# Seven products on token halves for half of a's rows, with weight sums by accumulating DMAs

## The chip, the core and the metric

The kernel runs on one core of one Trainium2 chip. The metric is the device time of one execution in microseconds; the median of 3 runs before the change is 2513.88 us.

## What is computed

Two layers of a model run one after the other on 512 tokens of 2048 channels, all in float32. Only the first part of the first layer matters here:

```python
h = rmsnorm(x, norm_g)
proj = jnp.einsum('bld,dn->bln', h, w_in)
v, bg, cg, za, u, zb, ga, gb = jnp.split(proj, SPLITS, axis=-1)
ya = bg * causal_depthwise_conv(cg * v, conv_w)
ya = jnp.einsum('blc,cd->bld', ya * jax.nn.silu(za), w_out_a)
yb = jax.nn.gelu(s5_scan(u, a_re, a_im, log_dt, b_re, b_im, c_re, c_im, d_skip))
```

The four parts v, cg, bg and za have 2048 channels each, and together they are "a". After them come the gate of the scan's output, the output projections, and the whole second layer; the change leaves those as they are but for their first loads and waits.

## The kernel before

Activations lie channel by token: a tile has 128 channels on the partitions and 512 tokens. Every matmul operand is split into a high part (rounded to the format TensorE takes, `hH`, `WH`) and a low part (the rest, `hL`, `WL`), and each product is three matmuls (`triple`, L560): high by high, high by low, low by high, added in PSUM.

The work is cut into **units**. A unit is one weight chunk of 128 x 1024 (512 KB): eight blocks of 128 x 128 for one output tile and half of the 2048 input channels, so 8 x 3 = 24 matmuls of 512 columns. An output tile (a projection) takes two units, kc 0 and 1. `Plan` (L69) writes the list of all units: u (8 tiles), zb (8), the gates ga and gb (32), then a in 16 blocks c of four tiles, then the rest. The first two u tiles are interleaved (kc 0 of both, then kc 1 of both); all others are in sequence.

Five queues go through the same list of units, each with a function `unit()`: SyncE loads the raw chunk into a ring of three slots `W` (`fetch`, L365), as soon as VectorE is done with the slot; ScalarE writes `WH` two units ahead (`hi`, L930, L936), when TensorE has left the buffer; VectorE writes `WL` (`lo`, L1304, L1307); TensorE waits for it (L557) and multiplies. Three buffers of `WH` and `WL` exist. Within a queue the order is the order in the program, so whatever stands between two calls of `unit()` delays the next split.

Around the change:

- At the start h is first computed without the token's factor (L998, L1602). VectorE and TensorE form the factor `RSA` meanwhile. POOL then scales x by it (L2181 to L2184), ScalarE writes the high parts again (`normed`, L1016, L1019) when the last u tile has read the old ones, and VectorE the low parts (L1634, L1636). The first zb tile waits for them, k by k (`n_ready`, L684).
- Beside the units runs the scan of u. `ssm_phases(n)` (L348) says how many of its phases each queue has done by unit n: one parameter piece per unit for units 4 to 24 (VectorE, `ssm_params`, L1413), then 130 phases up to the end of a's block `SSM_C` = 12 (units 28 to 199). In them POOL makes tables (L2138 to L2141), VectorE forms and scans (L1549 to L1578), TensorE drives and reads out (L603, L615).
- For each block c of a, the four tiles come as v, cg, bg and za; ScalarE copies the first out of PSUM (L1056), VectorE multiplies, convolves with three taps and multiplies (L1672 to L1691), ScalarE applies silu (L1061), and SyncE stores the product in DRAM (L454).

## Time and profile before

| | |
|---|---|
| median of 3 runs | 2513.88 us (2513.25 to 2514.46) |
| the profiled execution | 2516.84 us |
| its span | 2515.6 us |
| mean granted clock of TensorE | 0.998 |
| busy: TensorE, VectorE, ScalarE, POOL | 2496.6, 1592.1, 857.1, 369.9 us |
| bytes moved | 353.08 MB, mean 140 GB/s |

The durations of matmuls in the profile overlap, since the next one starts before the last has left the array; the distance between starts is what a matmul costs. The profile has one execution, 3 us above the median.

### The profile page before, as it was taken

To read this page: it belongs to the slowest core of one execution; us is meant where nothing else is said; L and a number is where in the kernel's file an instruction comes from. 1 tells how busy PE (TensorE), PEld (TensorE's weight loads), DVE (VectorE), ACT (ScalarE), POOL (GpSimd) and SP (SyncE) were. 2 spreads that over 40 slices of the span, in tenths; PEclk is the share of its full clock that TensorE was granted. 3 is DMA by queue.
4 is the path that set the end of the run, shared out by engine and by line. 5 is a ranking of instruction groups with operands and counts; after the bars stand their busy time and mean duration, and the time that the engine had idled before them with its cause. 6 is when DMAs were issued, how large, how long until landed. Compare 5 with 4: busy or idle time off the path is not lost.

```text
span 2515.6 us, 30050 instructions
## 1 busy us (share of the span) xinstructions
PE 2496.6 (99%) x11932; PEld 2158.8 (86%) x11932; DVE 1592.1 (63%) x2161; ACT 857.1 (34%) x1171; POOL 369.9 (15%) x286
## 2 busy tenths in 40 slices
PE   9899999999999999999999999999999999999998
PEld 8788888888888888888888888878888888888888
DVE  7976666668777777743756666557566564467534
ACT  5322222222222222223432223333465664324432
POOL 2133343334333343100000000000000000000001
PEclk9999999999999999999999999999999999999999
DMA  5243433333333333333576667524322222556333
GB/s 195 90 147 132 138 136 129 135 121 124 98 126 115 114 116 110 108 105 109 188 253 228 226 233 235 184 90 154 106 84 84 85 77 91 190 169 209 126 126 126
DMA packets 117964, 353.08 MB, mean 140 GB/s; under 512 B 15424, under 2 KB 18752, under 8 KB 117824
## 3 DMA queue, kind: packets, MB, share of 16 engines
q1 hardware_dynamic: 117824, 351.16, 41.5%
q8 instruction: 94, 1.54, 0.2%
q14 instruction: 46, 0.38, 0.0%
HBM read 321.68 MB, written 23.07 MB: 137 GB/s over the span
## 4 chain that ended last, share of the span: by engine, by line
PE 96%; DVE 2%; DMA 1%; ACT 0%; SPq 0%; issue 0%; DVEq 0%; ACTq 0%
PE bank L561 28%; PE bank L563 28%; PE bank L562 28%; PE bank L764 2%; PE bank L765 2%; PE bank L763 2%; PE bank L817 1%; PE bank L807 1%; PE bank L624 1%; PE bank L727 1%; PE bank L612 1%; DMA W<-in_w 1%; DVE WL L1307 0%; DVE SM L1394 0%; PE bank L800 0%; PE bank L798 0%
## 5 line engine op out<-in xcount | busy, mean ns | idle before, releaser
L1307 DVE TENSOR_TENSOR WL<-W,WH 128x1024 fp32r<-128x1024 f32 (+1 forms) x452 | 585.9, 1298 | 563.4 <-ACT WH L936 561.8
L936 ACT ACTIVATE WH<-W 128x1024 fp32r<-128x1024 f32 (+1 forms) x452 | 473.8, 1050 | 953.6 <-PE bank L563 671.7
L561 PE MATMUL bank<-hH,WH 128*128 128x512 f32 x1792 | 682.6, 381 | 8.6 <-DVE hL L1636 5.7
L563 PE MATMUL bank<-hH,WL 128*128 128x512 f32 x1792 | 680.5, 380 | 0.0
L562 PE MATMUL bank<-hL,WH 128*128 128x512 f32 x1792 | 680.4, 380 | 0.0
L561 PEld LDWEIGHTS bank<-hH,WH 128*128 128x128 f32 x1792 | 339.5, 189 | 67.8 <-issue 13.1
L563 PEld LDWEIGHTS bank<-hH,WL 128*128 128x128 f32 x1792 | 339.4, 189 | 48.4
L562 PEld LDWEIGHTS bank<-hL,WH 128*128 128x128 f32 x1792 | 339.6, 190 | 47.5
L561 PE MATMUL bank<-h2H,WH 128*128 128x512 f32 x624 | 239.6, 384 | 0.1
L562 PE MATMUL bank<-h2L,WH 128*128 128x512 f32 x624 | 236.5, 379 | 0.0
L563 PE MATMUL bank<-h2H,WL 128*128 128x512 f32 x624 | 236.5, 379 | 0.0
L2138 POOL TENSOR_TENSOR TAB<-E,W 128x512 f32<-128x512 f32 x64 | 84.0, 1313 | 537.9 <-DVE V L1576 519.4
L561 PEld LDWEIGHTS bank<-h2H,WH 128*128 128x128 f32 x624 | 117.9, 189 | 18.2 <-issue 1.4
L563 PEld LDWEIGHTS bank<-h2H,WL 128*128 128x128 f32 x624 | 117.9, 189 | 16.7
L562 PEld LDWEIGHTS bank<-h2L,WH 128*128 128x128 f32 x624 | 118.0, 189 | 15.8
L2141 POOL TENSOR_TENSOR TAB<-TAB,T 128x512 f32<-128x512 f32 x64 | 123.6, 1931 | 5.0
L1323 DVE SCALAR_TENSOR_TENSOR ACC<-W,SC,ACC 128x1024 f32<-128x1024 f32 x90 | 115.1, 1279 | 1.0 <-DMA W<-in_ada 0.6
L2192 POOL TENSOR_SCALAR YK<-X,PC,ST 128x512 f32<-128x512 f32 x16 | 12.8, 802 | 632.8 <-DVE X L1769 632.8
L763 PE MATMUL bank<-WH,h2H 128*128 128x512 f32 x256 | 97.6, 381 | 0.0
L561 PE MATMUL bank<-AH,WH 128*128 128x512 f32 x256 | 97.2, 380 | 0.0
L561 PE MATMUL bank<-mH,WH 128*128 128x512 f32 x256 | 97.2, 380 | 0.0
L562 PE MATMUL bank<-AL,WH 128*128 128x512 f32 x256 | 97.0, 379 | 0.0
(306 smaller groups left out, 3534.2 us busy)
## 6 DMA issues: line engine op xcount, KB each, us to landing
W<-in_w SPq DMA_DIRECT2D x332, 512.0 KB, 3.6
W<-in_ada SPq DMA_DIRECT2D x96, 512.0 KB, 4.1
W<-in_wa SPq DMA_DIRECT2D x32, 512.0 KB, 4.2
W<-in_wo SPq DMA_DIRECT2D x32, 512.0 KB, 3.7
W<-in_wvv SPq DMA_DIRECT2D x32, 512.0 KB, 4.1
W<-in_wb SPq DMA_DIRECT2D x16, 512.0 KB, 4.5
URAW<-U SPq DMA_DIRECT2D x96, 64.0 KB, 3.1
scr_ga<-SO SPq DMA_DIRECT2D x16, 256.0 KB, 2.0
```

The lines of the kernel that those rows point to most:

```text
L561: e.matmul(o, wh, xh, start=first, stop=False)
L562: e.matmul(o, wh, xl, start=False, stop=False)
L563: return e.matmul(o, wl, xh, start=False, stop=last)
L612: mm = e.matmul(bank[b + z][:, :], BSTK[:, s, z, :], pairs(USTK[:, s, :]), start=True, stop=True)
L763: e.matmul(o, h2H[:, k, q4[q]], wh, start=k == 0, stop=False)
L764: e.matmul(o, h2H[:, k, q4[q]], wl, start=False, stop=False)
L765: mm = e.matmul(o, h2L[:, k, q4[q]], wh, start=False, stop=k == 15)
L936: e.activation(chunk_parts(n)[0][:, c], W[:, i % NW, c], ACT.Copy).then_inc(sem["hi"], 1)
L1307: e.tensor_tensor(wl[:, c], W[:, plan.item_of[n] % NW, c], wh[:, c].bitcast(F32), ALU.subtract).then_inc(sem["lo_v"], 1)
L1323: e.scalar_tensor_tensor(out=acc[:, :], in0=w, scalar=c, in1=acc[:, :], op0=ALU.mult, op1=ALU.add).then_inc(sem["ada_v"], 1)
L2138: e.tensor_tensor(o, er_, wi if part else wr, ALU.mult).then_inc(sem["ssm_p"], 1)
L2141: e.tensor_tensor(o, o, y, ALU.add if part else ALU.subtract).then_inc(sem["ssm_p"], 1)
```

## The change

Three parts.

**The products.** For the blocks c = 8 to 15 of a, the 512 tokens and the 2048 input channels are each taken as two halves, and the four tiles as two pairs j, (cg, v) and (bg, za), by `ST_PARTS`. Each pair by both halves of channels is a 2 x 2 grid of weight chunks b11, b12, b21, b22, and each pair's result on both token halves is formed from seven products in place of eight. A unit i of a block is one product of 24 matmuls with 256 columns, for pair j = i % 2, so a block has 14 units in place of 8. The sums of the weights are not computed by an engine: for units 0 to 3 and 6 and 7 SyncE loads a plain chunk (`base`), and for units 4, 5 and 8 to 13 POOL issues a DMA with `accum_op=ALU.add`, which adds another chunk to what the slot holds, when VectorE has split the chunk before. Six raw slots are used, three of them new (`WX`). The sums of the tokens are formed once, in block c = 7, by VectorE and ScalarE (`factor_sums`), and the fourth goes in the place of the second token half of `hH` and `hL` for channels 0 to 1023. The partial results lie in three PSUM banks per pair, are copied out in the middle of the accumulation by ScalarE, and added by VectorE in `corner_11`, `corner_12` and `corner_22`.

**The scan** has to be finished before block 8: `SSM_C` is 6 in place of 12, so the same 130 phases go into units 28 to 151.

**The head.** The last two u tiles and the first two zb tiles are interleaved like the first two u tiles (`two_rows`, `project_two`). POOL's 16 scalings of x are VectorE's (`scaled_rows`), and the high and low parts are written in four groups of four with a `unit()` between.

The diff, cut to its core:

```diff
-SSM_C = 12
+SSM_C = 6
+ST_C = 8
+ST_PARTS = ((2, 0), (1, 3))
+ST_SLOTS = (0, 0, 1, 1, 0, 0, 2, 2, 0, 0, 2, 2, 0, 0)
...
+        self.two_rows("u", [[w1[64 + m, c] for c in range(2)] for m in range(2)])
+        for m in range(2, 6):
+            self.proj("u", [w1[64 + m, c] for c in range(2)])
+        self.two_rows("u", [[w1[64 + m, c] for c in range(2)] for m in (6, 7)])
+        self.two_rows("zb", [[w1[72 + m, c] for c in range(2)] for m in range(2)])
         for m in range(2, 8):
-            self.proj("u", [w1[64 + m, c] for c in range(2)])
-        for m in range(8):
             self.proj("zb", [w1[72 + m, c] for c in range(2)])
         for m in range(32):
             self.proj("gate", [w1[80 + m, c] for c in range(2)])
-        for c in range(16):
+        for c in range(ST_C):
             for part in (0, 2, 1, 3):
                 self.proj("a", [w1[16 * part + c, kc] for kc in range(2)])
+        self.strassen_units(w1)
...
+    def strassen_units(self, w1):
+        self.first_after = i0 = len(self.items)
+        slots = [[i0 % NW, (i0 + 1) % NW], [(i0 + 2) % NW, 3], [4, 5]]
+        user = dict(self.ring_user)
+        base, sums = [0] * 6, [0] * 6
+        for c in range(ST_C, 16):
+            n0 = len(self.item_of)
+            self.strassen[c] = n0
+            b = [[[w1[16 * part + c, kc] for part in ST_PARTS[j]] for kc in range(2)] for j in range(2)]
+            for i in range(14):
+                n, j = n0 + i, i % 2
+                s = slots[ST_SLOTS[i]][j]
+                self.item_of.append(None)
+                self.slot_of[n] = s
+                (b11, b12), (b21, b22) = b[j]
+                raw, added = ((b11, None), (b21, None), (None, b12), (b22, None), (None, b22), (None, b12),
+                              (None, b21))[i // 2]
+                if raw is not None:
+                    base[s] += 16
+                    self.base[c, i] = (s, raw, user.get(s))
+                    self.arrives[n] = ("base", s, base[s])
+                else:
+                    sums[s] += 16
+                    self.sums[c, i] = (s, added, user[s])
+                    self.arrives[n] = ("sum", s, sums[s])
+                user[s] = ("unit", n)
+            slots = slots[1:] + slots[:1]
...
+    def two_rows(self, stage, srcs):
+        n = [self.chunk(srcs[m][c]) for c in range(2) for m in range(2)]
...
+    def slot_free(user):
+        kind, i = user
+        return lo_done[i] if kind == "unit" else (sem["ada_v"], i + 1)
...
+    def r_bank(c, r, j):
+        return bank[(0, 1, 2, 4, 5, 6)[r + 3 * j] if r or c % 2 == ST_C % 2 else (3, 7)[j]]
+    MC = [SI[:, i // 2, half[i % 2]] for i in range(4)]
...
+        def base(c, i):
+            s, src, user = plan.base[c, i]
+            if user is not None:
+                e.wait_ge(*slot_free(user))
+            elif s > NW:
+                e.wait_ge(*nth("st_l", 0))
+            e.dma_start(raw_chunk(plan.strassen[c] + i), src).then_inc(w_base[s], 16)
+        def store_product(c):
+            e.wait_ge(*product_done[c])
+            e.dma_start(scratch["am"][c], SO[:, c % 2, :]).then_inc(spilled[c % 2], 16)
...
+        for c in range(ST_C):
             for _ in range(8):
                 ssm_until(unit())
-            e.wait_ge(*nth("a_v", c))
-            e.dma_start(scratch["am"][c], SO[:, c % 2, :]).then_inc(spilled[c % 2], 16)
+            if c < ST_C - 1:
+                store_product(c)
+        for i in (0, 1, 2, 3, 6, 7):
+            base(ST_C, i)
+        store_product(ST_C - 1)
+        for c in range(ST_C, 16):
+            if c < 15:
+                base(c + 1, 0)
+                base(c + 1, 1)
+            if c > ST_C:
+                store_product(c - 1)
+            if c < 15:
+                for i in (2, 3, 6, 7):
+                    base(c + 1, i)
+            for _ in range(14):
+                unit()
+        store_product(15)
...
+        def project_two(ps, XH, XL, ready=None, beside=None):
+            for kc in range(2):
+                for p in ps:
+                    n = unit()
+                    if beside is not None:
+                        beside(n)
+                    products(n, p, kc, 0, 15, XH, XL, ready if p == ps[0] else None)
...
-        for p in u_p[2:]:
+        for p in u_p[2:6]:
             project(p, xh, xl, beside=norm)
+        project_two(u_p[6:], xh, xl, beside=ssm_until)
         def n_ready(k):
             e.wait_ge(*nth("xl", 16 + k))
 
-        for i, p in enumerate(spill_p + a_p):
-            project(p, xh, xl, n_ready if i == 0 else None, beside=ssm_until)
+        project_two(spill_p[:2], xh, xl, n_ready, beside=ssm_until)
+        for p in spill_p[2:] + a_p:
+            project(p, xh, xl, beside=ssm_until)
+        first_half = lambda x, k0: (lambda k: x[:, k0 + k, half[0]])
+        second_half = lambda x, k0: (lambda k: x[:, k0 + k, half[1]])
+        whole = lambda x: (lambda k: x[:, k, :])
+        factors = [(first_half(hH, 0), first_half(hL, 0)), (first_half(hH, 8), first_half(hL, 8)),
+                   (whole(S1H), whole(S1L)), (second_half(hH, 0), second_half(hL, 0)),
+                   (whole(S2H), whole(S2L)), (whole(S3H), whole(S3L)), (second_half(hH, 8), second_half(hL, 8))]
+        def strassen_product(c, i):
+            f, j, g = i // 2, i % 2, c - ST_C
+            n = unit()
+            r = (0, 1, 2, 2, 0, 0, 0)[f]
+            if f == 0:
+                if c == ST_C:
+                    for w in conv_read[0] if j == 0 else [nth("skip", 7)]:
+                        e.wait_ge(*w)
+                elif c == ST_C + 1:
+                    e.wait_ge(*nth("skip", 7))
+                else:
+                    e.wait_ge(*nth("st_v", g - 2, (8, 13)[j]))
+            elif f == 1:
+                for w in [nth("st_v", g - 1, (1, 2)[j])] if g else conv_read[1] if j == 0 else []:
+                    e.wait_ge(*w)
+            elif f == 2:
+                for w in [nth("st_v", g - 1, (3, 6)[j])] if g else conv_read[2] if j == 0 else []:
+                    e.wait_ge(*w)
+                if g == 0:
+                    e.wait_ge(*nth("st_l", 0))
+            elif f == 3:
+                e.wait_ge(*nth("st_a", g, 3 + j))
+                if g == 0:
+                    e.wait_ge(*nth("s4_l", 0))
+            elif f == 4:
+                e.wait_ge(*nth("st_a", g, 1 + j))
+            elif f == 5:
+                e.wait_ge(*nth("st_a", g, 5 + j))
+            else:
+                e.wait_ge(*nth("st_v", g, (5, 7)[j]))
+            xh_, xl_ = factors[f]
+            o = r_bank(c, r, j)[:, 0:256]
+            for k8 in range(8):
+                w = slice(128 * k8, 128 * k8 + 128)
+                begins = f in (0, 1, 2) and k8 == 0
+                ends = f in (1, 3, 6) and k8 == 7
+                wh, wl, x_h, x_l = WH[:, n % NB, w], WL[:, n % NB, w], pairs(xh_(k8)), pairs(xl_(k8))
+                e.matmul(o, wh, x_h, start=begins, stop=False, skip_group_check=True)
+                e.matmul(o, wh, x_l, start=False, stop=False, skip_group_check=True)
+                mm = e.matmul(o, wl, x_h, start=False, stop=ends, skip_group_check=True)
+            mm.then_inc(sem["used"], 1)
+        for c in range(ST_C, 16):
+            for i in range(14):
+                strassen_product(c, i)
...
         def normed(k):
-            e.wait_ge(sem["used"], plan.last(u_p[7]) + k // 8)
+            e.wait_ge(sem["used"], plan.units(u_p[7])[k // 8] + 1)
             e.wait_ge(*nth("xn", k))
...
+        for i in range(4):
+            for k in range(4 * i, 4 * i + 4):
+                normed(k)
+            ssm_until(unit())
+        spill(0)
+        spill(1)
+        for s in range(2, len(spill_p)):
+            ssm_until(unit())
+            ssm_until(unit())
+            spill(s)
...
+        for c in range(ST_C, 16):
+            g = c - ST_C
+            for i in range(14):
+                if i in (1, 2, 5, 6, 9, 10):
+                    j = (i - 1) % 2
+                    m = j + 2 * (4 < i < 8)
+                    unit_done(c, i - 1)
+                    if i == 1 and g == 0:
+                        e.wait_ge(*nth("s4_l", 0))
+                    if g > 0 and i < 8:
+                        e.wait_ge(*nth("st_v", g - 1, (3, 6, 5, 7)[m]))
+                    if i > 8:
+                        e.wait_ge(*nth("st_v", g, 1 + j))
+                    e.activation(MC[m], r_bank(c, 2 if 4 < i < 8 else 0, j)[:, 0:256],
+                                 ACT.Copy).then_inc(sem["st_a"], 1)
+                unit()
...
+        def scaled_rows(ks):
+            for k in ks:
+                e.wait_ge(*nth("xsq", k))
+                e.wait_ge(*nth("xl", k))
+                e.tensor_tensor(XS[:, k, :], XS[:, k, :], RSA[:, :], ALU.mult).then_inc(sem["xn"], 1)
+        for m in range(3, 6):
             ssm_until(unit())
             if m == 4:
                 e.wait_ge(*nth("rsa", 0))
-                for i in range(4):
+                for i in range(2):
                     keep_u(i)
+            if m == 5:
+                keep_u(4)
+                scaled_rows(range(4))
             ssm_until(unit())
             if m == 3:
                 inv_rms(0, 3, 0, 0)
-            else:
-                keep_u(m)
+            if m == 4:
+                keep_u(2)
+                keep_u(3)
+            if m == 5:
+                scaled_rows(range(4, 8))
+        for i in range(4):
+            ssm_until(unit())
+            if i == 0:
+                keep_u(5)
+            scaled_rows(range(8 + 2 * i, 10 + 2 * i))
...
             ssm_until(unit())
-            if s == 0:
-                for k in range(8, 16):
-                    normed(k)
+            if i == 1:
+                keep_u(6)
+                keep_u(7)
...
+        def factor_sums(batch):
+            k, l = slice(4 * batch, 4 * batch + 4), slice(8 + 4 * batch, 12 + 4 * batch)
+            a, b, d, s4 = SX[0][:, :, :], SX[1][:, :, :], SX[2][:, :, :], SX4[batch][:, :, :]
+            if batch:
+                e.wait_ge(*nth("st_l", 0, 3))
+            for x, ks, h in ((a, k, 0), (b, k, 1), (d, l, 1), (s4, l, 0)):
+                e.tensor_tensor(x, f32(hH[:, ks, half[h]]), f32(hL[:, ks, half[h]]),
+                                ALU.add).then_inc(sem["st_x"], 1)
+            yield
+            e.wait_ge(*nth("st_x", 0, 8 * batch + 3))
+            e.tensor_tensor(d, d, b, ALU.subtract).then_inc(sem["st_x"], 1)
+            e.wait_ge(*nth("st_x", 0, 8 * batch + 5))
+            e.tensor_tensor(b, a, b, ALU.subtract).then_inc(sem["st_x"], 1)
+            e.wait_ge(*nth("st_x", 0, 8 * batch + 6))
+            e.scalar_tensor_tensor(out=a, in0=d, scalar=-1.0, in1=a, op0=ALU.mult,
+                                   op1=ALU.subtract).then_inc(sem["st_x"], 1)
+            e.wait_ge(*nth("st_x", 0, 8 * batch + 7))
+            e.scalar_tensor_tensor(out=s4, in0=s4, scalar=-1.0, in1=a, op0=ALU.mult,
+                                   op1=ALU.subtract).then_inc(sem["st_x"], 1)
+            yield
+            for f, (lo_, hi_, x) in enumerate(((S1L, S1H, d), (S3L, S3H, b), (S2L, S2H, a))):
+                e.wait_ge(*nth("st_h", 0, 3 * batch + f + 1))
+                e.tensor_tensor(lo_[:, k, :], x, f32(hi_[:, k, :]), ALU.subtract).then_inc(sem["st_l"], 1)
+            yield
...
+        def corner_22(c, j):
+            g = c - ST_C
+            unit_done(c, 10 + j)
+            e.wait_ge(*nth("st_a", g, 3 + j))
+            if g > 0:
+                e.wait_ge(*nth("st_v", g - 1, (8, 14)[j]))
+            o_ = x22[0] if j == 0 else halves(x22[1])
+            a, b = MC[2 + j], r_bank(c, 0, j)[:, 0:256]
+            e.tensor_tensor(o_, a if j == 0 else tokens(a), b if j == 0 else tokens(b),
+                            ALU.add).then_inc(sem["st_v"], 1)
...
+            if i == 10:
+                corner_12(c, 0)
+                e.wait_ge(*nth("st_v", g, 3))
+                e.wait_ge(*(nth("st_v", g - 1, 11) if g > 0 else nth("a_v", ST_C - 1, 4)))
+                e.tensor_tensor(halves(cv[:, half[0]]), tokens(x11[0]), tokens(x12[0]),
+                                ALU.mult).then_inc(sem["st_v"], 1)
+            if i == 11:
+                corner_22(c, 0)
+                corner_12(c, 1)
+            if i == 12:
+                corner_22(c, 1)
+            if i == 13:
+                unit_done(c, 12)
+                e.wait_ge(*nth("st_v", g, 5))
+                e.tensor_tensor(halves(cv[:, half[1]]), tokens(r_bank(c, 0, 0)[:, 0:256]), tokens(x22[0]),
+                                ALU.mult).then_inc(sem["st_v"], 1)
+                e.wait_ge(*nth("st_v", g, 8))
+                e.wait_ge(*(nth("st_v", g - 1, 14) if g > 0 else nth("a_v", ST_C - 1, 6)))
+                e.tensor_scalar(o, CV[:, 0:512], taps[0], None, ALU.mult).then_inc(sem["st_v"], 1)
+                for x in (1, 2):
+                    e.wait_ge(*nth("st_v", g, 8 + x))
+                    e.scalar_tensor_tensor(out=o, in0=CV[:, x:512 + x], scalar=taps[x], in1=o, op0=ALU.mult,
+                                           op1=ALU.add).then_inc(sem["st_v"], 1)
...
-        e.wait_ge(*nth("rsa", 0))
-        for k in range(16):
-            e.wait_ge(*nth("xsq", k))
-            e.wait_ge(*nth("xl", k))
-            e.tensor_tensor(XS[:, k, :], XS[:, k, :], RSA[:, :], ALU.mult).then_inc(sem["xn"], 1)
-        for n in range(4, plan.units(wg_p[0])[0]):
+        for n in range(4, plan.strassen[ST_C]):
             ssm_until(n)
         for _ in beside:
             pass
+        for c in range(ST_C, 16):
+            for i in (4, 5, 8, 9, 10, 11, 12, 13):
+                s, src, user = plan.sums[c, i]
+                e.wait_ge(*slot_free(user))
+                e.dma_start(raw_chunk(plan.strassen[c] + i), src, accum_op=ALU.add).then_inc(w_sum[s], 16)
```

## Rows read from the trace of the kernel before

**Rows 1.** The page: TensorE's busy time, its clock in 40 slices, the chain

```profile
PE 2496.6 (99%) x11932; PEld 2158.8 (86%) x11932; DVE 1592.1 (63%) x2161; ACT 857.1 (34%) x1171; POOL 369.9 (15%) x286
...
PEclk9999999999999999999999999999999999999999
...
PE 96%; DVE 2%; DMA 1%; ACT 0%; SPq 0%; issue 0%; DVEq 0%; ACTq 0%
```

**Rows 2.** Timeline, TensorE, 512 wide: start, length, engine, line; 73 starts apart

```profile
2459.84 0.38 PE L561 MATMUL bank<-yH,WH 128*128 128x512 f32 x1
...
2475.60 0.38 PE L562 MATMUL bank<-yL,WH 128*128 128x512 f32 x1
```

**Rows 3.** Timeline, TensorE, 256 wide, 48 starts apart

```profile
2485.92 0.28 PE L561 MATMUL bank<-yH,WHX 128*128 128x256 f32 x1
...
2491.28 0.28 PE L561 MATMUL bank<-yH,WH 128*128 128x256 f32 x1
```

**Rows 4.** Windows: length, busy by engine, granted clock, DMA share, GB/s

```profile
400.00:800.00 400.00, 400.00 (x1881) 344.40 (x1880) 290.85 (x330) 103.21 (x129) 143.28 (x100) 1.00 0.36 121
800.00:1000.00 200.00, 200.00 (x941) 172.21 (x940) 153.61 (x175) 50.28 (x61) 72.65 (x52) 1.00 0.34 113
```

**Rows 5.** Groups by form, 560 to 1210 us: busy us, mean ns

```profile
L1307 DVE TENSOR_TENSOR WL<-W,WH 128x1024 fp32r<-128x1024 f32 x122 | 168.6, 1382 | 134.9 <-ACT WH L936 134.3
...
L1557 DVE TENSOR_TENSOR V<-V 128x512 f32<-128x512 f32 x18 | 12.5, 692 | 0.5
...
L936 ACT ACTIVATE WH<-W 128x1024 fp32r<-128x1024 f32 x123 | 129.7, 1055 | 373.6 <-PE bank L563 373.6
```

**Rows 6.** DMA: a window at full load; issues, KB, us to landing

```profile
10.00:12.00 2.00, 2.00 (x11) 1.67 (x11) 1.78 (x3) 1.29 (x3) 0.00 (x0) 1.00 1.06 409
...
W<-in_w SPq DMA_DIRECT2D x332, 512.0 KB, 3.6
...
XS<-in_xT SPq DMA_DIRECT2D x7, 512.0 KB, 8.6
```

**Rows 7.** Chain of waits, 40 to 115 us: start us, length, what

```profile
58.82 1.21 DVE SM L1394
...
95.64 0.61 DVE T L1391
...
99.89 0.69 DVE U L1619
100.59 5.30 DVE hL L1636 x8
105.88 1.14 DVE WL L1307
107.02 0.61 DVE T L1391
...
108.57 0.76 DVE hL L1636
```

**Rows 8.** Waits of TensorE: total us, times, longest

```profile
PE bank L561 <- DVE hL L1636: 5.7, 2, 3.1
```

**Rows 9.** Timeline, TensorE, at 75 us; in brackets its idle time

```profile
75.67 0.48 PE L561 MATMUL bank<-hH,WH 128*128 128x512 f32 x1 [2.63 <-DVE WL L1307]
...
77.88 0.63 PE L561 MATMUL bank<-hH,WH 128*128 128x512 f32 x1
78.31 0.63 PE L562 MATMUL bank<-hL,WH 128*128 128x512 f32 x1
```

**Rows 10.** POOL scaling x, and a small operation of VectorE after it

```profile
L2184 POOL TENSOR_TENSOR XS<-XS,RSA x16: 1267/1276/2265, 53.1 to 73.3; 128x512 f32<-128x512 f32 x16
...
75.95 0.19 DVE L1391 TENSOR_TENSOR SM<-SM,SMI 128x32 f32<-128x32 f32 x1
```

**Rows 11.** Timeline, VectorE: ends of the next parameter piece

```profile
115.01 0.18 DVE L1491 COPY SM<-SM 128x32 f32<-128x32 f32 x1
...
118.22 0.18 DVE L1386 TENSOR_SCALAR SM<-SM 128x32 f32<-128x32 f32 x1
```

More of the change, by code:

```diff
@@ L1663, in dve_program @@
                     ssm_until(unit())
-                if c == 15 and i >= 2:
-                    for k in range(4 * (i - 2), 4 * (i - 2) + 4):
-                        low_y(k)
+                    if c == ST_C - 1:
+                        next(factors, None)
+                if c == ST_C - 1 and i == 3:
+                    last_factor_low(0)
+                    last_factor_low(1)
                 if i == 1:
@@ L1693, in gate_in @@
+        for c in range(ST_C, 16):
+            for i in range(14):
+                unit()
+                if i == 0 and c > ST_C:
+                    gated_conv(c - 1, 14)
+                if i in (3, 4):
+                    corner_11(c, i - 3)
+                if i >= 10:
+                    gated_conv(c, i)
+                if c == 15 and i >= 6:
+                    low_y(i - 6)
+        gated_conv(15, 14)
         def gate_in(i):
```

205 lines of the change are left out of this document (158 added, 47 removed).

## The prediction

> **What bounds the kernel now.** I read the page's busy times first. TensorE is busy for 2496.6 of 2515.6 us, at a granted clock of nine tenths or more in all 40 slices, and the chain that ended last is 96% PE [rows 1]. So the time is the count of matmuls times the interval between their starts, plus the few stalls, and a change pays only if it shortens one of the two.
>
> The interval is in the timeline, not in the durations, which overlap. 512-wide starts lie (2475.60 - 2459.84) / 73 = 0.216 us apart [rows 2]; 256-wide ones, which exist only near the end, (2491.28 - 2485.92) / 48 = 0.1117 us [rows 3]. Half the columns cost a little more than half the time, and the weight load beside each matmul does not show at 256.
>
> The other engines have room, but not everywhere. In the stage of the spilled rows and the first rows of a VectorE is busy 291 of 400 us, later 154 of 200 [rows 4]. Splitting one chunk costs ScalarE 1.06 us and VectorE 1.2 to 1.4 us [rows 5]. In the first 115 us the chain leaves TensorE and runs over VectorE [rows 7]: one stall of 2.63 us at 73 us, and two, 5.7 us in all, before the low parts of the second normalisation [rows 8, 9].
>
> **Part 1, the products: -30.** A unit is 24 matmuls. Before, a channel block c of 8 to 15 is 8 units of 24 x 0.2158 = 5.18 us, 41.4 us. After, 14 units of 24 x 0.1117 = 2.68 us, 37.5 us. Gain 3.9 us, times 8 = 31.3 us.
>
> Work beside it: splits now come every 2.68 us. ScalarE: 14 x 1.06 plus six copies and a gate, some 18 of 37.5 us. VectorE: 14 x 1.2, six corner sums and the convolution, some 24 us (256 wide taken as 0.35 to 0.4, half of the 0.69 of a 512-wide addition [rows 5]). Both fit. Where the two meet: unit 12 of a block overwrites a bank that VectorE must have read, and VectorE queues that read behind the split of unit 13. From the end of unit 10: ScalarE 1.06, VectorE 1.2, sum 0.4 and some 0.1 of signals make 2.8 us, against the 2.68 of unit 11. So 0.13 us of stall per block, 1 us in all. -31.3 + 1 = -30.
>
> **The DMAs** decide whether this holds. Every unit needs 512 KB: 6 plain loads and 8 accumulating ones per block. At full load the engines moved 409 GB/s [rows 6], so 512 KB take 1.28 us. No row shows an accumulating DMA. Lower bound: like a plain one. Upper bound: no row gives one. I take double, 2.56 us, since it reads the weights and the tile. The block then asks for (6 + 16 + 0.5 for the stored product) x 1.28 = 29 of 37.5 us. Latency: a sum starts when the slot's last split is done, 2.4 us into a unit (ScalarE 1.06, VectorE 1.2, signals [rows 5]), and is due four units later, so it may take 4 x 2.68 - 2.4 = 8.3 us. A plain load lands in 3.6 us [rows 6]; plus 1.3 for the second read, plus an estimated 1 on POOL, is 6, and 7.3 when a plain load is between. Cost: 0, covered by these 8.3 us. If the cover is gone, every us later is a us of stall per block, in unit 12 first.
> The Trainium skill, Collectives: The Full Stack, "Why ReduceScatter is half of AllGather", says an add in the DMA path halves the rate because it has two reads; no row here shows it, and it would give the same 2.56 us.
>
> The queues. SP loads units 0 and 1 of the next block first, then waits for the stored product of the block before (about 1 us into the block), and only behind it come units 2, 3, 6 and 7 of the next block, whose slots come free in units 8 to 11; they are due from the next block's start on, 7 us or more later. POOL issues the sums in order of the splits that release them, and behind the scan's tables, which end with c = 6. So neither queue holds a load back: 0.
>
> **Part 2, the head.** POOL loses its 16 scalings of 1.27 us [rows 10]. While they ran, VectorE's 128x32 operations took 1.21 us, else 0.19 [rows 7, 10], and that made the stall at 73 us. It goes: -2.6 us, and the half-speed matmuls behind it too (0.43 us apart [rows 9], some 8 of them, -1.6 us). Sum -4.2.
>
> But VectorE does the scalings itself now, 16 x 0.61 = 10 us (a 512-wide operation [rows 7]), in units 10 to 15, where its parameter pieces, splits and readings of u already fill nearly 24 of 31 us. It comes 1.7 us later to the last piece before unit 16, the one of 4.3 us, and has two scalings behind that. The first low part came 3 us after TensorE wanted it; now 4.3. The pairing doubles the time for each half in principle. But the four groups of low parts are each behind a unit of VectorE's, that is a split and a parameter piece. Group 2: split 1.15, piece 1.55 [rows 7], behind four low parts at 0.67 [rows 7], against half a unit: 2.8 us late. Group 3: a split that waits for the end of unit 16 (2.2 with ScalarE's part), a piece of 3.4 [rows 11], two readings of u, a low part, against 5.2 us of unit 17: 2.5 late. Group 4: four low parts, split, a piece of the same operations (some 2.7, an estimate), a low part, against half a unit: 3.8 late. Stalls: 4.3 + 2.8 + 2.5 + 3.8 = 13.4, less the 5.7 of before: +7.7. One more drop of the clock: +1.6. Between the bounds "both waits hidden" (-5.7) and +12 I take +9.3, as it comes from the same order that gives the old stalls right.
>
> **Part 3, the scan in fewer units.** It must now end with c = 6: 130 phases over 124 units instead of 172. VectorE's busy share less the splits (1.38 of 5.18 us, 0.27) is 0.50 in its later stretch [rows 4, 5], of which the convolution is about 0.1; 0.4 x 172 / 124 = 0.55, so 0.92 in all. It fits, with little left; the last readout lies one unit, not two, behind the phase that it waits for. +2, bounds 0 and +16 (every late readout).
>
> **Part 4, c = 7 and the ends.** The token sums are 22 operations of 1024 elements at 1.15 to 1.2 plus 2 more splits, 28 us beside splits and convolution (14) in 41: a lag of up to 5 us, under the 8 us that a split may come late at 512 width. 0, bound +4. One us for the two ends of the stage.
>
> **Sum:** -30 - 4.2 + 9.3 + 2 + 1 = -22 us. The profiled execution took 2516.84 us (span 2515.6), 3.0 above the median 2513.88; I put the same -22 on the median: 2492 us. Its own range is 2480 to 2505.
>
> **Rivals.**
> **A, sums that land late (slower, 0.27).** Place: the accumulating DMA of unit 13, the last of six in a row, one per 2.68 us. If one costs three plain ones, 3.84 us, the row gains 1.16 us each, and it lands after 6 + 1.3 + 5 x 1.16 = 13 us, plus the next block's loads. Against 8.3 that is 5 to 7 us per block: -30 + 8 x 6 + 8 (parts 2 to 4) = +26, 2540 us. It decides from about 11 us on, where the 30 us less the 8 are used up (3.8 - 1 = 2.8 us per block); then 2514. For it: no row shows such a DMA, and under full load at the start plain loads of 512 KB took 8.6 us to land [rows 6]. Against: a demand of 29 us in 37.5. With the clock falling after each stall, as it did after 2.63 us [rows 9], it could be 2580.
> The same could come from POOL's side: rows 7 and 10 show VectorE and POOL holding each other up, and VectorE is busy two thirds of this stage. One operation of 1.2 us ahead of each issue gives 7.2 to 8.5 us of latency, at most 0.2 us of stall; three give 11. The Trainium skill, SBUF — State Buffer, "SBUF: two separate sides", says that POOL's descriptors wait only for VectorE's two-port operations; the block has one of those, and by that rule nothing is lost.
> **B, VectorE bounds the first 900 us (0.13).** Its slowed operations (a split at 1.38 instead of 1.15 in mean [rows 5]) grow with POOL's share, which rises by 1.39 too. Part 3 at its bound: -22 + 14 + 3 = -5, 2509 us.
> **C, both waits of the head are hidden (0.10).** That is -5.7 - 1.6 instead of +9.3: -38, 2476 us. Against: the order above.
> That the change does not do what it says has no room: 14 products of 256 columns stand in the loop.
>
> **Numbers.** Forecast 0.50. About 0.2% (5 us) is what a measurement tells from none. Faster: 0.48 of the forecast, 0.10 of C, 0.04 of B = 0.62. Same: 0.02 + 0.05 of B + 0.03 of A = 0.10. Slower: 0.04 of B, 0.24 of A = 0.28. The range from 2475 to 2545 leaves out half of A above 2540 and a little of C.
>
> **What would show it.** Right: 256-wide starts 0.112 us apart in the a stage, blocks of about 37.7 us, landing of the accumulating DMAs under 8 us, VectorE's small operations at 0.19 us before 75 us, four stalls before low parts between 98 and 125 us. Wrong: TensorE waiting for splits or corner sums inside the blocks, blocks over 41 us, the chain running over DMA or VectorE in the a stage, no stall at 98 us.

## The result, and the profile after

The changed kernel takes 2498.45 us in the median of four runs (2498.32 to 2498.74); the kernel before, run beside it, takes 2514.17 us. The ratio is 0.9936, interval 0.9919 to 0.9953: 15.7 us or 0.6% faster, where the forecast was 2492 and 22 us. The profiled executions took 2516.84 and 2498.38 us.

The page of the changed kernel: busy times, four lines of the slices, the software DMA queue, the chain by engine.

```profile
span 2497.2 us, 32838 instructions
PE 2469.8 (99%) x13084; PEld 2171.9 (87%) x13084; DVE 1721.4 (69%) x2313; ACT 925.9 (37%) x1267; POOL 410.4 (16%) x334
...
PE   9799999999999999999999999999999999999998
...
DVE  7877889789999875666856666557565554467534
...
PEclk9899999999999999999999999999999999999999
DMA  5244444343333379988676677524222222556333
...
q0 software_dynamic: 9216, 33.56, 7.6%
...
PE 94%; DVE 3%; issue 1%; ACT 1%; DMA 1%; SPq 0%; DVEq 0%; ACTq 0%
```

Against [rows 1] TensorE's busy time fell by 26.8 us and the span by 18.4: more matmul time was saved than reached the end. The second slice shows where the rest went. Its PE digit is 7 and its clock digit 8, and the whole chain has 3% on VectorE, where it had 2% [rows 1]. The slices are 62 us wide, so this is the stretch from 62 to 125 us.

What TensorE waited for in the whole kernel (line, what it waited for, us in total, times, longest):

```profile
PE bank L690 <- DVE hL L1896: 7.7, 2, 4.5
PE bank L690 <- DVE U L1862: 6.6, 1, 6.6
PE bank L794 <- POOL CAU L2577: 2.0, 1, 2.0
PE bank L876 <- DVE T L2035: 1.9, 8, 0.4
```

The two waits for low parts [rows 8] have become 4.5 and 3.2 us, and a new one of 6.6 us stands between them: TensorE waits for VectorE to write U. The stall at 73 us [rows 9] is gone. TensorE's timeline, rows of 512 columns:

```profile
98.16 0.77 PE L690 MATMUL bank<-hH,WH 128*128 128x512 f32 x1 [4.50 <-DVE hL L1896]
98.72 0.63 PE L691 MATMUL bank<-hL,WH 128*128 128x512 f32 x1
99.14 0.63 PE L692 MATMUL bank<-hH,WL 128*128 128x512 f32 x1
...
112.96 0.77 PE L690 MATMUL bank<-hH,WH 128*128 128x512 f32 x1 [6.56 <-DVE U L1862]
...
116.50 0.47 PE L692 MATMUL bank<-hH,WL 128*128 128x512 f32 x1
116.81 0.38 PE L690 MATMUL bank<-hH,WH 128*128 128x512 f32 x1
117.02 0.38 PE L691 MATMUL bank<-hL,WH 128*128 128x512 f32 x1
...
126.03 0.48 PE L690 MATMUL bank<-hH,WH 128*128 128x512 f32 x1 [3.23 <-DVE hL L1896]
```

Behind the first two waits the starts lie 0.43 us apart, half speed, for 13 and 9 matmuls (the first and last of them in part), before they are 0.216 apart again; behind the third, three matmuls run at full speed and then 9 are slow. Against full speed this costs 2.85, 1.9 and 1.7 us, 6.5 us in all. Such a stretch does not follow every wait. In the kernel before, two of three waits had one, of 1.7 us each, and this one had none:

```profile
101.39 0.45 PE L561 MATMUL bank<-hH,WH 128*128 128x512 f32 x1 [3.05 <-DVE hL L1636]
101.68 0.38 PE L562 MATMUL bank<-hL,WH 128*128 128x512 f32 x1
```

VectorE's timeline says why the wait of 6.6 us exists:

```profile
102.69 2.74 DVE L1896 SCALAR_TENSOR_TENSOR hL<-XS,PC,hH 128x512 fp32r<-128x512 f32 x4
107.58 1.23 DVE L1551 TENSOR_TENSOR WL<-W,WH 128x1024 fp32r<-128x1024 f32 x1 [2.15 <-ACT WH L1130]
108.72 0.17 DVE L1734 COPY SM<-SM 128x32 f32<-128x32 f32 x1
...
112.12 1.29 DVE L1862 TENSOR_TENSOR U<-bank,RSA 128x512 f32<-128x512 f32 x2
113.33 2.73 DVE L1896 SCALAR_TENSOR_TENSOR hL<-XS,PC,hH 128x512 fp32r<-128x512 f32 x4
```

Unit 17, the second row of the zb pair, takes the PSUM bank that u row 6 left. VectorE reads that bank (`keep_u(6)`) only after the split of unit 19, which waits for the end of unit 16, and after the parameter piece from 108.7 to 112.1 us. Before, u row 6 was finished one unit earlier (units 12 and 13 instead of 12 and 14) and read at 88.09 us, and its bank was taken one unit later, by unit 18.

In the blocks of seven products the timeline shows 256-wide starts, with one gap per block, before unit 12:

```profile
956.73 0.28 PE L876 MATMUL bank<-S3H,WH 128*128 128x256 f32 x1
...
961.64 0.28 PE L878 MATMUL bank<-S3H,WL 128*128 128x256 f32 x1
962.14 0.35 PE L876 MATMUL bank<-hH,WH 128*128 128x256 f32 x1 [0.22 <-DVE T L2035]
```

Forty-four intervals between the first two rows make 0.1116 us each, as in [rows 3]. The gap from start to start is 0.50 instead of 0.11 us, so it costs 0.39. The gate activation of a block comes every 38.00 us (1002.73, 1040.73, 1078.73 us), against 41.43 us per block before (192 starts; the gate activations behind the scan, at 1131.21 and 1172.65 us, lie 41.44 apart): 8 x 3.43 = 27.4 us.

The accumulating DMAs, by their line (durations on POOL in ns, then landing):

```profile
L2588 POOL DMA_DIRECT2D W<-in_w x35: 858/865/1028, 889.3 to 1176.8; - x35
...
DMA to landing us min/median/max: 5.3/6.0/8.0
```

The landing times are of all 64 sums, in `W` and `WX`. The one that can delay unit 12 is the sum of unit 13, the last of six. It landed in 6.0 to 7.5 us; the 8.0 was a sum of unit 5. How long it may take is in the timelines: its issue, and the split that uses it, which starts when TensorE has freed the buffer.

```profile
951.23 0.86 POOL L2588 DMA_DIRECT2D WX<-in_w  x1 [1.13 <-DVE WL L1551]
...
959.33 1.07 ACT L1130 ACTIVATE WH<-WX 128x1024 fp32r<-128x1024 f32 x1 [0.89 <-PE bank L878]
```

That is 8.1 us, in the last block too (1179.23 to 1187.33), where the sum landed after 7.5.

The stretch from 900 to 1180 us of the kernel before (busy time of PE, PEld, DVE, ACT, POOL, then clock, DMA share, GB/s):

```profile
900.00:1180.00 280.00, 280.00 (x1311) 242.24 (x1311) 166.77 (x189) 66.66 (x75) 49.07 (x34) 1.00 0.33 110
```

and the same stretch of the changed kernel:

```profile
900.00:1180.00 280.00, 278.44 (x2480) 277.31 (x2479) 170.54 (x205) 133.28 (x167) 53.54 (x62) 1.00 0.90 196
```

The DMA engines are busy 90% of this stage, nearly full, and yet TensorE loses 1.6 us of 280.

### The profile page after: what moved, and what is told of

The parts are those of the page before. It is cut to its first block, busy times and chain, and to the rows that moved or that the text cites. A ratio compares the mean times of both kernels' runs of the same rounds, so it can differ in the third digit from the quotient of the medians.

```text
span 2497.2 us, 32838 instructions
## 1 busy us (share of the span) xinstructions
PE 2469.8 (99%) x13084; PEld 2171.9 (87%) x13084; DVE 1721.4 (69%) x2313; ACT 925.9 (37%) x1267; POOL 410.4 (16%) x334
## 4 chain that ended last, share of the span: by engine, by line
PE 94%; DVE 3%; issue 1%; ACT 1%; DMA 1%; SPq 0%; DVEq 0%; ACTq 0%
PE bank L690 24%; PE bank L691 24%; PE bank L692 24%; PE bank L876 4%; PE bank L878 4%; PE bank L877 4%; PE bank L958 2%; PE bank L959 2%; PE bank L960 2%; PE bank L1012 1%; PE bank L1002 1%; DVE WL L1551 1%; DMA W<-in_w 1%; PE bank L762 1%; ACT WH L1130 1%
## 5 line engine op out<-in xcount | busy, mean ns | idle before, releaser
L690 PE MATMUL bank<-hH,WH 128*128 128x512 f32 x1280 | 489.7, 383 | 15.1 <-DVE hL L1896 7.7
L691 PE MATMUL bank<-hL,WH 128*128 128x512 f32 x1280 | 487.6, 381 | 0.0
L692 PE MATMUL bank<-hH,WL 128*128 128x512 f32 x1280 | 487.1, 381 | 0.0
L692 PEld LDWEIGHTS bank<-hH,WL 128*128 128x128 f32 x1280 | 243.3, 190 | 35.0
L691 PEld LDWEIGHTS bank<-hL,WH 128*128 128x128 f32 x1280 | 243.5, 190 | 34.2
L876 PE MATMUL bank<-hH,WH 128*128 128x256 f32 x512 | 141.5, 276 | 1.9 <-DVE T L2035 1.9
L877 PE MATMUL bank<-hL,WH 128*128 128x256 f32 x512 | 140.8, 275 | 0.0
L878 PE MATMUL bank<-hH,WL 128*128 128x256 f32 x512 | 140.8, 275 | 0.0
L2541 POOL TENSOR_TENSOR TAB<-TAB,T 128x512 f32<-128x512 f32 x64 | 113.5, 1773 | 5.0
L1551 DVE TENSOR_TENSOR WL<-WX,WH 128x1024 fp32r<-128x1024 f32 x53 | 65.0, 1226 | 54.0 <-ACT WH L1130 54.0
```

The costliest lines, as they stand in the source:

```text
L690: e.matmul(o, wh, xh, start=first, stop=False)
L691: e.matmul(o, wh, xl, start=False, stop=False)
L692: return e.matmul(o, wl, xh, start=False, stop=last)
L876: e.matmul(o, wh, x_h, start=begins, stop=False, skip_group_check=True)
L877: e.matmul(o, wh, x_l, start=False, stop=False, skip_group_check=True)
L878: mm = e.matmul(o, wl, x_h, start=False, stop=ends, skip_group_check=True)
```

## The experiments

Two theories stood after this reading: that the products bring 27 us and the head takes 9 to 10 back, and that the loss is elsewhere (denser scan, accumulating DMAs, ends of the stage). Ratios are to the kernel before, run in the same rounds (its medians there: 2515.4 to 2516.6 us). Differences to the changed kernel are between medians of different rounds, where the kernel before took 2514.17 us, so they can be off by 1 to 2.5 us.

**The head of before, with the products.** Edit: plan, TensorE, ScalarE and VectorE loops of the head and POOL's scalings as in the kernel before; the rest as changed.

```diff
-        for m in range(2, 6):
+        for m in range(2, 8):
             self.proj("u", [w1[64 + m, c] for c in range(2)])
-        self.two_rows("u", [[w1[64 + m, c] for c in range(2)] for m in (6, 7)])
-        self.two_rows("zb", [[w1[72 + m, c] for c in range(2)] for m in range(2)])
-        for m in range(2, 8):
+        for m in range(8):
             self.proj("zb", [w1[72 + m, c] for c in range(2)])
...
```

> The changed kernel with the head of before: u and zb one row after the other, the scalings on POOL, the readings of u where they were. Theory (products -27.4, head +9): the two parts add up, so this is the changed kernel less 9 us, 2489.5, ratio to before 0.9902; stalls of 2.6 us at 73 us and 5.7 us before low parts as in before, no wait of 6.6 us for a bank, blocks c = 8 to 15 still 38.0 us. By the sum of the prediction (head +5.1) it would be 2493. Rival (the head is harmless, the missing microseconds are lost elsewhere, for instance where the scan has fewer units): the same time as the changed kernel, 2498.

2487.91 us, ratio 0.989 [0.9877, 0.9904]: 27.7 us less than before and 10.5 less than the changed kernel. The waits are those of before (low parts 5.7 us in 2; a split 2.6), and blocks last 38.0 us. The products alone bring the 27.4 us that their blocks show; within the interval nothing is lost at the ends of the stage.

**The new head alone,** on the kernel before.

> The kernel before with the head of the change alone (rows 6 and 7 of u and 0 and 1 of zb in pairs, the scalings on VectorE, the readings of u in their new places); no Strassen, the scan in as many units as before. Theory (the head costs 9 us by itself): 9 us slower than before, ratio 1.0036, with the waits 4.5, 6.6 and 3.2 us near 98, 113 and 126 us. Rival (the head costs only beside the denser scan or the other loads of the changed kernel): no change, ratio 1.000.

2525.40 us, ratio 1.0036 [1.0023, 1.0048], 9.65 us slower than before. Its waits:

```profile
PE bank L567 <- DVE hL L1676: 8.6, 3, 4.5
PE bank L567 <- DVE U L1642: 6.6, 1, 6.6
```

The waits of 4.5, 6.6 and 3.2 us are there without any product or denser scan, and one of 0.93 us more, before low parts at 103.31 us: here the half-speed stretch behind the first wait has 8 slow starts and not 13, and TensorE comes early enough to wait again. Behind the 3.2 us there is no slow stretch. The head costs this by itself, and -27.7 + 9.65 = -18.0 agrees with the -15.7 measured, given intervals of 3 to 4 us either way. It is one bundle: no run has the pairing without the scalings on VectorE.

**Reading u rows 6 and 7 earlier.**

```diff
+            if i == 1:
+                keep_u(6)
+                keep_u(7)
             ssm_until(unit())
-            if i == 1:
-                keep_u(6)
-                keep_u(7)
```

> The changed kernel with the readings of u rows 6 and 7 (keep_u) before the split and the parameter piece of their unit instead of behind them. Theory (unit 17 waits 6.6 us for the bank of u row 6 alone): that wait goes; low parts 8 to 11 come 1.3 us earlier and then stall unit 18 by 1.2 us, low parts 12 to 15 stall by 4.1 instead of 3.2 us; with a little of the clock back, 4.5 to 6 us less than the changed kernel, 2493. Rival (unit 17 is also held by its split or by other low parts, the bank is only the last in name): under 1 us less.

2492.61 us, ratio 0.9908 [0.9894, 0.9921], 5.8 us less than the changed kernel. The wait for U is gone, and those for low parts are now 10.4 us in 4 instead of 7.7 in 2. It was the bank that held unit 17; part of the time went to the next low parts (1.5 us more at 113 us, 3.6 at 120 us), as worked out.

**Plain DMAs in place of accumulating ones.**

```diff
-                e.dma_start(raw_chunk(plan.strassen[c] + i), src, accum_op=ALU.add).then_inc(w_sum[s], 16)
+                e.dma_start(raw_chunk(plan.strassen[c] + i), src).then_inc(w_sum[s], 16)
```

> The changed kernel with the 64 accumulating DMAs turned into plain ones on the same queue, at the same places and with the same waits; it leaves out the second summand of the seven weight sums, so rows c = 8 to 15 of a are not the reference's. Theory (the DMAs are covered): no change of time, within 1 us of the changed kernel; landing falls from 6.0 us to about 4.5, the queue's share of the engines to about half. Rival (the accumulation in SBUF slows splits or matmul operands in the blocks, 38.0 instead of 37.7 us each): 2 to 3 us less.

2498.73 us, no change. The line that issues the DMAs, as above:

```profile
L2588 POOL DMA_DIRECT2D W<-in_w x35: 527/527/751, 888.6 to 1176.1; - x35
...
DMA to landing us min/median/max: 3.6/4.4/5.3
```

the queue, on its page:

```profile
q0 software_dynamic: 9216, 33.56, 4.2%
```

and the stretch from 900 to 1180 us:

```profile
900.00:1180.00 280.00, 278.40 (x2479) 277.27 (x2479) 170.82 (x206) 133.29 (x168) 33.35 (x61) 1.00 0.61 197
```

The queue's share of 16 engines falls from 7.6 to 4.2% of the span: 2.97 us of all engines for one accumulating DMA of 512 KB, 1.64 for a plain one. The blocks stay at 38.0 us, so a DMA share of 0.90 or 0.61 makes no difference to TensorE here, where nothing lands late.

**The corner sum ahead of the split.**

```diff
+                if i == 11:
+                    corner_22(c, 0)
                 unit()
...
-                corner_22(c, 0)
                 corner_12(c, 1)
```

> The changed kernel with the corner sum that frees the bank of unit 12 put before VectorE's split of unit 13 instead of behind it. Theory (unit 12 waits 0.22 us per block for that sum, because the sum queues behind a split that itself waits for the end of unit 10): the eight waits go, 1.8 us less, 2496.7; blocks 37.8 us. Rival (unit 12 or 13 then waits for its split instead, as the sum now delays it): no change.

2498.72 us, no change: the rival. Unit 12 no longer waits, but unit 13 does:

```profile
965.12 0.35 PE L876 MATMUL bank<-hH,WH 128*128 128x256 f32 x1 [0.22 <-DVE T L2035]
```

Its bank is freed by the sister sum, which queues behind the split of unit 14 in the same way. The 0.39 us in front of unit 12 had hidden that; it now stands in front of unit 13, and the blocks last 37.97 us. With both sums moved (below) the blocks take 37.52 us.

**The scan in fewer units, alone,** in the kernel before (`SSM_C = 12` becomes 6).

> The kernel before with the scan to be done with channel block 6 instead of 12 (130 phases over 124 units instead of 172), nothing else. Theory (VectorE has room, no wait of TensorE seen between 140 and 892 us in the changed kernel): 0, within 1 us of before. By the sum of the prediction +2, at its bound +16, 2530.

2515.97 us, ratio 1.000 [0.9991, 1.0009]. VectorE's share rises to what it is in the changed kernel (371 of 400 us busy between 400 and 800, [rows 4] had 291), and TensorE waits for nothing there.

**Sums that are released later.** Three runs, one, two or three units later:

```diff
-                e.wait_ge(*slot_free(user))
+                e.wait_ge(*slot_free((user[0], user[1] + 1)))
```

> The changed kernel with each of the 64 accumulating DMAs issued two units (5.4 us) later: POOL waits for the split of the unit two behind the one that frees the slot. Theory (a late sum holds the splits, and these have two more units less their own 2.3 us before TensorE needs them, so the cover is 8.3 + 3.1 = 11.4 us and not the 8.3 of the prediction): a landing of 6.0 us still fits in the 6.0 us that are left, so 0 to 8 us more than the changed kernel, under 2507. Rival (the prediction's cover of 8.3 us): 2.9 us are left, 3.1 us are lost at least three times per block, 74 us more, 2573.

> The same, three units (8.0 us) later. Theory (cover 11.4 us): 3.4 us are left for a landing of 6.0, so 2.6 us are lost in each of the three steps from sum to sum of a block, units 4, 8 and 12: some 8 us per block, 64 us in all, 2562, more where the clock falls behind the stalls. Rival (cover 8.3 us): 5.7 us at each step, 17 per block, 2635.

2658.32 us (ratio 1.0567) and 2922.23 us (1.1614), 20 and 53 us more per block. Both theories fell: a cover of 11.4 us gave at most 2507 and 2562, one of 8.3 us gave 2573 and 2635. Both had added up single steps, though a sum released two units late waits for the split of a unit that itself waits for a sum (the sum of unit 10 for the split of unit 8, that of 12 for 10). And 65 us of the first run's waits were `T`, the corner sum behind the split of unit 13, the place the prediction had named (51 us more were splits). These two runs show the place; the size of the cover, 8.1 us, is from the trace of the changed kernel above.

> The changed kernel with each accumulating DMA issued one unit (2.7 us) later. After the runs with two and three units: theory now (the sum of unit 13 has a cover of 8.3 us, because its split stands ahead of the corner sum that unit 12 waits for; the other seven have 11.4): unit 13 has 5.6 us left for a landing of 6.0 to 6.8 us, a queue model of the block with these gives 0.9 to 2.5 us per block, 7 to 20 us in all, 2505 to 2519. Rival (all eight have 11.4 us, the losses of the two runs come only from sums that wait for one another): nothing lost, 2499. Other rival (all eight have 8.3 us): 0.4 to 1.2 us in each of three steps, but TensorE waits before units 4, 8 and 12 alike.

2570.68 us, ratio 1.0222 [1.0206, 1.0237]: 9.0 us per block, over 3 times the upper end of the model. TensorE's waits in it:

```profile
PE bank L876 <- DVE T L2035: 41.6, 8, 6.2
PE bank L876 <- DVE WL L1551: 8.0, 12, 1.6
```

POOL's timeline in one block:

```profile
952.50 0.86 POOL L2588 DMA_DIRECT2D W<-in_w  x1 [8.82 <-DVE WL L1551]
953.96 0.86 POOL L2588 DMA_DIRECT2D WX<-in_w  x1 [0.60 <-DVE WL L1551]
955.52 0.86 POOL L2588 DMA_DIRECT2D W<-in_w  x1 [0.69 <-DVE WL L1551]
...
965.89 0.86 POOL L2588 DMA_DIRECT2D WX<-in_w  x1 [1.73 <-DVE WL L1551]
```

and the split of unit 13 in ScalarE's timeline, 7.8 us behind its issue:

```profile
973.70 1.06 ACT L1130 ACTIVATE WH<-WX 128x1024 fp32r<-128x1024 f32 x1 [2.68 <-DMA WX<-in_w]
```

Three releases come in a bunch, behind a split of unit 5 that waited for its own sum. The first of the three, issued at 952.50, landed after 5.6 us, the third (unit 10's, 955.52) after 7.7. Unit 10's split had to wait for it:

```profile
963.28 1.06 ACT L1130 ACTIVATE WH<-W 128x1024 fp32r<-128x1024 f32 x1 [1.02 <-DMA W<-in_w]
```

That split releases unit 13's sum, so this one was issued late too, and landed 7.8 us after its issue at 965.89. Over the eight blocks unit 13's sums took 7.8 to 9.5 us, where the changed kernel has 6.0 to 7.5. Waits for `T` and splits are 49.6 us, 47.7 more than the 1.9 of the changed kernel; 21 of the other 24 us are 198 starts of matmuls that lie up to twice as far apart (granted clock 0.94 between 890 and 1260 us). What kind of queueing lengthens the landing was not separated.

**Products for four blocks only** (`ST_C = 8` becomes 12).

> The changed kernel with the products for channel blocks 12 to 15 only (ST_C = 12), blocks 8 to 11 with 512 columns again. Theory (the gain is 3.4 us per block and linear in the blocks): four blocks fewer give back 13.7 us, 2512 us; the four that are left last 38.0 us each. Rival (part of the gain or loss sits at the ends of the stage or in the room that the freed DMA time gives): more than 3 us off that.

2512.49 us, ratio 0.9984 [0.9975, 0.9993]: 14.0 us more than the changed kernel by the medians, 12.1 by the ratios, so 3.0 to 3.5 per block. Within what rounds differ by, the gain is linear in the blocks.

**A version with the head put right.**

```diff
+PARAM_LATE = {14: 1, 15: 2, 16: 3, 17: 4, 18: 4, 19: 4, 20: 3, 21: 3, 22: 2, 23: 2, 24: 1}
...
-        for i in range(4):
-            for k in range(4 * i, 4 * i + 4):
+        for ks in ((4, 8), (8, 16), (), ()):
+            for k in range(*ks) if ks else ():
                 normed(k)
...
-            while done[0] < ssm_phases(n):
+            while done[0] < ssm_phases(n) - PARAM_LATE.get(n, 0):
...
+            if i == 3:
+                keep_u(6)
+            if i >= 2:
+                for k in range(4 * (i - 2), 4 * (i - 2) + 4):
+                    normed(k)
...
+                if i in (11, 12):
+                    corner_22(c, i - 11)
                 unit()
```

> The changed kernel with three things moved: low parts ahead of the parameter pieces of units 14 to 17 on VectorE, these pieces being made up for by unit 25; the high parts for the second normalisation 4, 4 and 8 in a row on ScalarE, ahead of the splits that wait for TensorE; the readings of u rows 6 and 7 ahead of unit 17 and behind the low parts; both corner sums that free a bank ahead of the split. Theory (each wait of the head is VectorE's order, not its load): the waits near 98, 113 and 126 us and the half-speed matmuls behind them go, 14.3 us of waits and 2 to 4 us of clock, and 2 us in the blocks: 2479 to 2482. Rival (VectorE has no room for the deferred pieces before the scan begins): the waits come back between 120 and 170 us, 2488 or more.

2479.34 us, ratio 0.9852 [0.9839, 0.9865]: 19.1 us less than the changed kernel by the medians (21 by the ratios) and 37 less than before. Its waits:

```profile
PE bank L751 <- DVE BSTK L1769: 3.5, 1, 3.5
PE bank L795 <- POOL CAU L2586: 2.0, 1, 2.0
```

The stretch of the head in it (columns as above):

```profile
95.00:105.00 10.00, 10.00 (x48) 8.77 (x47) 8.44 (x12) 6.55 (x10) 0.00 (x0) 1.00 0.33 107
105.00:115.00 10.00, 10.00 (x49) 8.74 (x47) 8.74 (x23) 2.30 (x5) 0.00 (x0) 1.00 0.33 103
```

Against the same stretches of the changed kernel:

```profile
95.00:105.00 10.00, 6.74 (x19) 5.02 (x20) 9.83 (x16) 2.26 (x4) 0.00 (x0) 0.66 0.14 52
105.00:115.00 10.00, 3.44 (x12) 2.50 (x12) 7.21 (x22) 3.51 (x5) 0.00 (x0) 0.74 0.16 52
```

TensorE runs through at full clock. The waits were in VectorE's order and not in its load, but one of 3.5 us has appeared at 144 us, before the scan's first drive. The moves were made together; apart from the reading of u, above, what each brings was not measured.

> The version with the three things moved (x9_best), and in addition the low parts of the first two B stacks two parameter pieces earlier on VectorE. Theory (its one wait of 3.5 us, before the first drive of the scan at 144 us, is for those stacks, which queue behind the pieces that are made up for): the wait goes with the clock behind it, 4 to 5 us less, 2474 to 2476. Rival (VectorE itself is late at that place, by its load): the wait moves to the first readings of the scan or to the splits near 160 us, 1 us less at most.

Edit: `stack_low(0)` and `stack_low(1)` at parameter piece 15 instead of 17. 2478.76 us, ratio 0.9857 [0.984, 0.9873], the same within the interval. The wait moved, as the rival had it:

```profile
PE bank L691 <- DVE WL L1556: 3.6, 2, 2.6
```

The stack was only the last in a queue. VectorE is busy 53.2 of the 60 us from 140 on, so there its load is probably the bound; no run takes work away from it there.

## Why the prediction was right and where it was off

- **Products, -30: measured -27.4 to -27.7.** Interval, unit and count were right. The term that was mis-sized is the stall before unit 12: 0.13 us forecast, 0.39 measured from start to start (2.1 us over eight blocks); some 0.1 us per block more lies right behind it, at the first matmuls of units 12 and 13. Its mechanism, the corner read queued behind the split of unit 13, was right; that unit 13 has the same wait right behind it was not seen.
- **DMAs at nothing: right.** Landing 6.0 us in the median where 6 to 7.3 was forecast. Unit 13's sums took up to 7.5 us, and the forecast 8.3 that they may take is 8.1 in the trace: it held by 0.6 us, a margin that the cost of 0 does not show. An accumulating DMA takes 1.81 times the engine time of a plain one beside it (2.97 to 1.64 us). The forecast had 2.56 to 1.28, so the factor of two held and both prices were too low: the stage asks for 90% of the DMA engines, not the forecast 29 of 37.5 us, 77%. The Trainium skill, Collectives: The Full Stack, "Why ReduceScatter is half of AllGather", says of that collective that its add halves the rate by needing two reads; 1.81 agrees with that roughly. POOL's issues took 0.86 us with a largest of 1.03, beside a VectorE busy 61% of the time, so none was held up by an operation of 1.2 us. The Trainium skill, SBUF — State Buffer, "SBUF: two separate sides", has POOL's descriptors wait only for VectorE's two-port operations; these issues do not contradict it, and no run puts it to the test.
- **Head, stall at 73 us gone: right** (-2.6, and VectorE's small operations at 0.17 to 0.19 us once POOL does no scalings).
- **Head, four stalls of 4.3, 2.8, 2.5 and 3.8: two came in place and size** (4.50 and 3.23), both with some luck. The 4.3 does not follow from the terms beside it: 3.05 of before, 1.7 later, two scalings 1.2, less a reading of u 0.6, make 5.3. In the traces VectorE begins the last piece (at 91.72 us; 95.56 before) 1.94 us before TensorE wants the low part instead of 2.78, so 0.8 later and not 1.7, and 3.05 + 0.84 + 1.21 - 0.61 = 4.5. Before the fourth stall the forecast had VectorE busy with four low parts; it was idle for 5.34 us, until ScalarE's split at the end of unit 17 (split at 121.40, low parts from 125.22).
- **The second stall** did not come, because behind the first stall TensorE lost 2.85 us at half speed and reached those low parts later: the half speed took the place of the 2.8 us, and where the slow stretch was shorter, in the run with the new head alone, 0.93 us of the stall came back.
- **The third stall** was another one. Unit 17 was not stopped by low parts but by the bank of u row 6, 6.6 us. The step "Group 3: a split that waits for the end of unit 16, a piece of 3.4, two readings of u, a low part" had the right queue, but counted only the low part at its end and did not ask who waits for the two readings in it.
- **The head in all.** The waits add to 14.3 us against 13.4 forecast, since what the bank cost (+4.1) and the stall that did not come (-2.8) nearly cancel. The term that failed by more is "One more drop of the clock: +1.6". With the one at 73 us gone, it counts two drops of 1.6, as many as before; there were three, of 6.5 us together against 3.4 before, 3 us more where the forecast had none. That the clock had not fallen behind one of the two old waits for low parts, the 3.05 us at 101.39, was in the trace. With the gain at 73 us the head is +9.65 where +5.1 was forecast.
- **Scan in fewer units, +2: 0.** The load estimate was right (0.92 forecast, 371 of 400 us measured); the late readout did not show.
- **Part 4 and the ends, +1: 0.** TensorE waits for nothing in block c = 7, nor at the start of the stage behind the blocks.
- **The total** was 6 us too hopeful: +4.5 on the head, +2.5 on the products, -3 on scan and ends; the rest, 2 us, is within what two medians of before differ by. The misses partly cancel; without the 3 us it would have been 9.
- **Rival A** named the right place, but its condition, "decides from about 11 us on", has the price too low. In the run one unit later unit 13's sums landed after 7.8 to 9.5 us, with the 2.7 us of delay like a landing of 10.5 to 12.2; the block lost 9.0 us there, where one us of stall per us late gives 2 to 4, and the run was 55 us slower than before instead of about even with it. The price left out that late sums release later sums late and in a bunch, and the clock. What was a chance of 0.27 hung on less than 2.7 us of cover.
- **Rival B:** no, by the run with the scan's deadline alone. **Rival C:** not in this order, but the last versions show it as a possible one: 2479, near its 2476.

## What to carry to other kernels

When a unit of work is moved forward, list everything that must be free for it, the PSUM bank as well as the operands, and look at where each release stands in its engine's queue; an operation placed behind a split and a filler piece is as late as both. Give each stall of TensorE its own price for the half-speed matmuls that may follow it (here 1.7 to 3.0 us behind most stalls of 2.6 to 6.6 us, and nothing behind others of 2.6 to 3.2), not one for all, and ask what a slow stretch hides: it took the place of the next stall. And of a transfer that is hidden, give the cover and not only the cost, for the transfer with the least: here 7.5 of 8.1 us were used at worst, and one unit later cost 72 us.

## What the runs showed of the hardware

- A DMA of 512 KB with an addition in SBUF takes 0.86 us to issue on POOL and 6.0 us to land, the plain one on the same queue 0.53 and 4.4 us, in a stage where the engines are 90 and 61% busy. It takes 2.97 and 1.64 us of the 16 engines.
- A wait of TensorE for another engine costs more than the profile's figure for the wait: 0.22 us before unit 12 puts the starts 0.50 us apart instead of 0.11, so it costs 0.39.
- Half speed does not follow every stall. Stalls of 2.63, 2.62, 4.50 and 6.56 us were followed by 8 to 13 starts 0.43 us apart; in the kernel before one of 3.05 us was not, nor was the 3.23 us of the run with the new head alone, though the same 3.23 us in the changed kernel was.
- Where POOL starts on the scan's tables, VectorE and POOL slow each other. In the version with the head put right VectorE's splits take 1.23 us until 152 us and 1.6 us each (two in 3.21 us) at 158.75 us; POOL's table operations beside them take 2.09 and 2.03 us, and 1.05 us ten microseconds later. The Trainium skill, SBUF — State Buffer, "SBUF: two separate sides", has the two share a port pair exclusively, also where VectorE reads two operands in SBUF and POOL reads SBUF; these rows agree.
